# Expert weights in 16 KB runs: gate and up as whole matrices, with the contraction permuted to match

## The reference

```python
lg = jnp.einsum('nd,dg->ng', xn, rg_w) + rg_b          # group of 4, top 1
le = (jnp.einsum('nd,de->ne', xn, re_w) + re_b).reshape(-1, N_GROUPS, EXPERTS_PER_GROUP)
...                                                     # top 2 of the 8 experts in it
for e in range(N_EXPERTS):
    hdn = jax.nn.silu(xn @ w_gate[e]) * (xn @ w_up[e])  # 1024 x 512 each
    out = out + combine[:, e:e + 1] * (hdn @ w_down[e]) # 512 x 1024
return x + out
```

## Time and profile before

| | us |
|---|---|
| median of 3 runs | 843.48 |
| the profiled execution | 843.39 |
| its span | 841.6 |
| TensorE matmuls busy | 775.0 (92%) |
| VectorE busy | 427.2 (51%) |
| ScalarE busy | 324.3 (39%) |
| TensorE waiting for `exp_w_up` transfers | 26.3 |
| SP weight transfers, issue to landing, median | 25.9 to 26.9 |

### The profile page before, as it was taken

How to read it: one execution, slowest core, us unless ns; L and a number is a source line. 1 busy time by engine, 2 the same in 40 slices (tenths; PEclk the granted TensorE clock), 3 DMA queues, 4 the chain that set the end, 5 groups by cost and what they waited for, 6 DMA issues and landing times.

```text
span 841.6 us, 21589 instructions
## 1 busy us (share of the span) xinstructions
PE 775.0 (92%) x8655; PEld 591.7 (70%) x8656; DVE 427.2 (51%) x1142; ACT 324.3 (39%) x562; POOL 259.1 (31%) x132
## 2 busy tenths in 40 slices
PE   4999999999999999999999979999898889989964
PEld 4999999999999999865555545555555545545532
DVE  3156977999994244153444333445343334434424
ACT  4432767564345833253323322323322223222224
POOL 3846699978577778200000000000000000000000
PEclk9999999999999999989999999999999999999997
DMA  7734343435454746963899999999999999999992
GB/s 254 229 106 145 101 151 100 151 100 160 129 180 158 280 150 241 339 278 151 340 422 423 421 422 422 422 421 422 422 422 421 422 422 422 421 422 423 421 421 119
DMA packets 53173, 249.99 MB, mean 297 GB/s; under 512 B 6600, under 2 KB 6600, under 8 KB 28562
## 3 DMA queue, kind: packets, MB, share of 16 engines
q1 hardware_dynamic: 49760, 246.95, 74.1%
q10 hardware_dynamic: 3377, 2.57, 1.2%
HBM read 246.76 MB, written 2.75 MB: 296 GB/s over the span
## 4 chain that ended last, share of the span: by engine, by line
PE 62%; DMA 18%; DVE 11%; SPq 4%; ACT 2%; issue 2%; ACTq 1%; DVEq 0%
PE bank L1450 24%; DMA piece<-in_exp_w_up 17%; PE bank L1621 12%; DVE bank L1065 7%; PE bank L1650 7%; PE bank L1572 5%; PE bank L1609 4%; PE bank L1448 4%; SPq L549 4%; PE bank L1637 1%; DVE sq L1127 1%; PE bank L1579 1%; PE bank L1519 1%; DMA stage<-in_norm_g 1%; PE bank L1513 1%
## 5 line engine op out<-in xcount | busy, mean ns | idle before, releaser
L603 POOL TENSOR_TENSOR w_lo<-raw,w_hi 128x2048 fp32r<-128x2048 f32 x39 | 180.5, 4631 | 62.6 <-ACT w_hi L728 62.5
L1621 PE MATMUL bank<-piece,xe 128*32 128x256 f32 x2816 | 169.5, 392 | 32.1 <-DMA piece<-in_exp_w_up 26.3
L1621 PEld LDWEIGHTS bank<-piece,xe 128*32 128x32 f32 x2816 | 97.7, 113 | 98.0 <-issue 47.5
L1450 PE MATMUL bank<-x_hi,w_hi 128*128 128x384 f32 x432 | 145.4, 337 | 0.3 <-DVE ua L1084 0.2
L1450 PE MATMUL bank<-x_hi,w_lo 128*128 128x384 f32 x432 | 144.4, 334 | 0.0
L1450 PE MATMUL bank<-x_lo,w_hi 128*128 128x384 f32 x432 | 144.4, 334 | 0.0
L1065 DVE SCALAR_TENSOR_TENSOR bank<-ub,vec,bank 128x256 f32<-128x256 f32 (+1 forms) x416 | 137.2, 419 | 0.0
L1296 DVE SCALAR_TENSOR_TENSOR silu_and_hid<-bank,few,silu_and_hid 64x256 f32<-64x256 f32 x44 | 21.5, 490 | 170.4 <-ACT silu_and_hid L914 170.4
L728 ACT ACTIVATE w_hi<-raw 128x2048 fp32r<-128x2048 f32 x39 | 74.8, 1919 | 74.8 <-PE bank L1450 71.2
L1650 PE MATMUL bank<-piece,hidT 128*32 128x256 f32 x1408 | 94.2, 384 | 5.5
L1450 PEld LDWEIGHTS bank<-x_hi,w_hi 128*128 128x128 f32 x432 | 81.1, 188 | 1.4 <-DVE ua L1084 0.5
(11 more groups left out here) (239 smaller groups left out, 1009.9 us busy)
## 6 DMA issues: line engine op xcount, KB each, us to landing
piece<-in_exp_w_down SPq DMA_DIRECT2D x64, 1024.0 KB, 26.6
piece<-in_exp_w_gate SPq DMA_DIRECT2D x64, 1024.0 KB, 25.9
piece<-in_exp_w_up SPq DMA_DIRECT2D x64, 1024.0 KB, 26.9
raw<-in_w_in SPq DMA_DIRECT2D x28, 1024.0 KB, 5.2
raw<-in_w_out_a SPq DMA_DIRECT2D x4, 1024.0 KB, 5.0
raw<-in_w_out_b SPq DMA_DIRECT2D x4, 1024.0 KB, 5.3
raw<-in_w_o SPq DMA_DIRECT2D x4, 1024.0 KB, 5.0
out<-n_out SPq DMA_DIRECT2D x3, 512.0 KB, 3.3
```

What stands on the lines that cost most here:

```text
L603: pool.tensor_tensor(w_lo[u % NW][:, :, :], raw[u % NW][:, :, :], w_hi[u % NW][:, :, :].bitcast(F32), ALU.subtract).then_inc(lo_ready, 1)
L1450: ins = pe.matmul(b, wp[:, k % UK, cols], xp[:, k, :], start=start, stop=stop)
L1621: last = pe.matmul(GU[q * T:(q + 1) * T, :], xe[:, k, :], wide(pairs[q // 2], k)[:, q % 2 * QE:(q % 2 + 1) * QE], start=(k == 0), stop=(k ...
```

## The change

Gate and up of a side get one buffer of 16 KB per partition each, `matrix{n}`, which covers two adjacent pieces; down keeps its two pieces. The numbers in `SETS` change so that the two pieces of gate, and of up, are adjacent. In memory a matrix is now read as one contiguous block of 2 MiB in which partition `p` holds rows `8p` to `8p+7`, one run of 16 KB. Block `k` of the contraction is made of the rows `8 p + k`, and `by_row` and the load of `norm2_g` follow. For the first four experts each matrix is still loaded as two transfers of 8 KB per partition, now with a distance of 16 KB between the runs in memory. From the fifth expert on gate and up are one transfer each. `gate_up_half` is gone: both are issued on `gate_up_done`, and TensorE waits for both whole matrices in front of the first of its 64 matmuls.

```diff
-    SETS = (((15, 16), (17, 18), (20, 9)), ((10, 11), (12, 1), (2, 0)),
-            ((4, 7), (5, 8), (3, 6)), ((13, 14), (19, 21), (22, 23)))
+    SETS = (((16, 17), (10, 11), (15, 18)), ((0, 1), (4, 5), (9, 12)),
+            ((2, 3), (6, 7), (8, 13)), ((20, 21), (22, 23), (14, 19)))
...
+        matrix = {s[c][0]: at(f"matrix{s[c][0]}", [P, 4096], F32, halves_at + UNIT * s[c][0]) for s in SETS for c in range(2)}
...
-        w_gu = {0: w_gate.rearrange("l e (h p j) c -> (l e) h p (j c)", h=2, p=P),
-                1: w_up.rearrange("l e (h p j) c -> (l e) h p (j c)", h=2, p=P)}
+        w_gu = {0: w_gate.rearrange("l e (p j) c -> (l e) p (j c)", p=P), 1: w_up.rearrange("l e (p j) c -> (l e) p (j c)", p=P)}
...
-            return t.rearrange("p (h q j) -> p h j q", h=2, q=P)
+            return t.rearrange("p (q j) -> p j q", q=P)
...
-            return piece[pair[k // RJ]][:, :].rearrange("p (j c) -> p j c", j=RJ)[:, k % RJ, :]
+            return matrix[pair[0]][:, :].rearrange("p (k c) -> p k c", k=KB)[:, k, :]
...
-                for c, h in ((0, 0), (1, 0), (0, 1), (1, 1), (2, 0), (2, 1)):
-                    n = SETS[side][c][h]
-
-                    used = (down_half, down_done) if c == 2 else (gate_up_half, gate_up_done)
-                    sp.wait_ge(used[h], last_item)
-                    src = w_dn if c == 2 else w_gu[c]
-                    sp.dma_start(piece[n][:, :], src[bass.ds(e, 1), h, :, :].rearrange("e p x -> p (e x)"))\
+                sp.wait_ge(gate_up_done, last_item)
+                for c in range(2):
+                    n = SETS[side][c][0]
+                    sp.dma_start(matrix[n][:, :], w_gu[c][bass.ds(e, 1), :, :].rearrange("e p x -> p (e x)"))\
+                      .then_inc(weights_in[n], 16)
+                for h, done in enumerate((down_half, down_done)):
+                    n = SETS[side][2][h]
+                    sp.wait_ge(done, last_item)
+                    sp.dma_start(piece[n][:, :], w_dn[bass.ds(e, 1), h, :, :].rearrange("e p x -> p (e x)"))\
                       .then_inc(weights_in[n], 16)
...
-                for part, done in enumerate((gate_up_half, gate_up_done)):
-                    pe.wait_ge(weights_in[pairs[0][part]], filled)
-                    pe.wait_ge(weights_in[pairs[1][part]], filled)
-                    for k in range(part * KB // 2, (part + 1) * KB // 2):
+                pe.wait_ge(weights_in[pairs[0][0]], filled + 16)
+                pe.wait_ge(weights_in[pairs[1][0]], filled + 16)
+                for k in range(KB):
...
-                    last.then_inc(done, 1)
+                last.then_inc(gate_up_done, 1)
```

More of the change, by code:

```diff
@@ L56, in trunk_program @@
     HALF = 512
-    SETS = (((15, 16), (17, 18), (20, 9)), ((10, 11), (12, 1), (2, 0)),
-            ((4, 7), (5, 8), (3, 6)), ((13, 14), (19, 21), (22, 23)))
+    SETS = (((16, 17), (10, 11), (15, 18)), ((0, 1), (4, 5), (9, 12)),
+            ((2, 3), (6, 7), (8, 13)), ((20, 21), (22, 23), (14, 19)))
+    assert all(a % 2 == 0 and b == a + 1 for s in SETS for a, b in s[0:2])
     NSETS = len(SETS)
@@ L357, in trunk_program @@
         xe_ready = sem("xe_ready")
-        gate_up_half = sem("gate_up_half")
         gate_up_done = sem("gate_up_done")
@@ L481, in _, with first_weights @@
             sp.dma_start(x_tok[:, NP // P, :], x_sample.rearrange("s t d -> (s t) d")).then_inc(x_sample_in, 16)
[L483 to L488, removed]
+            FIRST = {SETS[e][c][h]: (e, c, h) for e in range(NSETS) for c in range(3) for h in range(2)}
+            def first_weights(*pieces):
+                for n in pieces:
+                    e, c, h = FIRST[n]
+                    if c == 2:
+                        sp.dma_start(piece[n][:, :], w_dn[e, h]).then_inc(weights_in[n], 16)
+                    else:
+                        m = SETS[e][c][0]
+                        sp.dma_start(matrix[m][:, h * 2048:(h + 1) * 2048], w_gu[c][e][:, h * 2048:(h + 1) * 2048])\
+                          .then_inc(weights_in[m], 16)
+            TAPS_USED = {32: 15, 33: 16, 34: 17, 35: 18}
             X_LO_USED = CHUNKS.index(("gB", 1))
@@ L491, in _ @@
                 if u == 30:
-                    first_weights(0, 2, 0)
+                    first_weights(20)
                 if u == 1:
@@ L503, in _ @@
                     sp.wait_ge(tails_ready, 2 + 4 * KB)
-                    first_weights(0, *TAPS_USED[u])
+                    first_weights(TAPS_USED[u])
             sp.wait_ge(grp_done, CHUNK_END[X_LO_USED])
-            first_weights(0, 2, 1)
+            first_weights(9)
             sp.wait_ge(grp_done, CHUNK_END[NCH - 3])
-            first_weights(1, 0, 0)
-            first_weights(1, 0, 1)
-            first_weights(1, 1, 0)
+            first_weights(10, 11, 12)
             sp.wait_ge(lo_ready, UNITS - 2)
-            first_weights(1, 1, 1)
+            first_weights(1)
             sp.wait_ge(lo_ready, UNITS - 1)
-            first_weights(1, 2, 0)
+            first_weights(2)
             sp.wait_ge(lo_ready, UNITS)
-            first_weights(1, 2, 1)
+            first_weights(0)
             sp.wait_ge(grp_done, CHUNK_END[NCH - 2])
-            first_weights(2, 0, 0)
-            first_weights(2, 0, 1)
+            first_weights(4, 7)
             sp.wait_ge(half_done, NCH)
-            first_weights(2, 1, 0)
-            first_weights(2, 1, 1)
+            first_weights(5, 8)
             sp.wait_ge(grp_done, len(GROUPS))
[L525 to L528, removed]
+            first_weights(3, 6, 13, 14)
             sp.wait_ge(aux_done, aux("logit", NT - 1) + 1)
-            first_weights(3, 1, 0)
+            first_weights(19)
             sp.wait_ge(stage_out[0], 80)
@@ L864, in _ @@
             act.dma_start(rw[:, :, NG:R], expert_w.rearrange("l (k p) g -> p (l k) g", p=P)).then_inc(rw_in, 16)
-            act.dma_start(norm2_by_row[:, :].rearrange("p (h j) -> p h j", h=2),
-                          norm2_g.rearrange("l (h p j) -> p (l h) j", h=2, p=P)).then_inc(rw_in, 16)
+            act.dma_start(norm2_by_row, norm2_g.rearrange("l (p j) -> p (l j)", p=P)).then_inc(rw_in, 16)
             act.dma_start(rbias[:, 0:NG], group_b.to_broadcast([P, NG])).then_inc(rw_in, 16)
@@ L878, in rows_in_blocks @@
             def rows_in_blocks(i):
-                act.activation(x_rows[:, i, :].rearrange("p (h j q) -> p h j q", h=2, j=RJ), by_row(x_tok[:, i, :]),
+                act.activation(x_rows[:, i, :].rearrange("p (j q) -> p j q", j=KB), by_row(x_tok[:, i, :]),
                                ACT.Copy).then_inc(x_rows_ready, 1)
@@ L1615, in item @@
                 pe.wait_ge(xe_ready, i + 1)
-                for part, done in enumerate((gate_up_half, gate_up_done)):
-                    pe.wait_ge(weights_in[pairs[0][part]], filled)
-                    pe.wait_ge(weights_in[pairs[1][part]], filled)
-                    for k in range(part * KB // 2, (part + 1) * KB // 2):
[L1620 to L1623, removed]
-                    last.then_inc(done, 1)
+                pe.wait_ge(weights_in[pairs[0][0]], filled + 16)
+                pe.wait_ge(weights_in[pairs[1][0]], filled + 16)
+                for k in range(KB):
+                    for q in range(TILES):
+                        last = pe.matmul(GU[q * T:(q + 1) * T, :], xe[:, k, :],
+                                         wide(pairs[q // 2], k)[:, q % 2 * QE:(q % 2 + 1) * QE],
+                                         start=(k == 0), stop=(k == KB - 1))
+                last.then_inc(gate_up_done, 1)
                 pe.wait_ge(picked, i + 2)
```

6 lines of the change are left out of this document (1 added, 5 removed).

## The result

The changed kernel takes 845.37 us in the median of 14 runs (841.98 to 846.39), the kernel before 843.61 in 14 runs beside them (843.2 to 844.99). The ratio is 1.0016, with a 95% interval of 1.0008 to 1.0023: slower by 0.16%, some 1.4 us. The forecast was 842.5, a gain of 0.9. The profiled execution took 844.6 us with a span of 842.8 (before: 843.39 and 841.6).

The account below looks back on a forecast made before the run. The prediction took the expert stage's weight stream as the bound, with TensorE's work behind its last gate/up bytes. From 843.39 it added 1.72 (start), -4.4 (rate), 1.73 (tail) and 0.1 (small edits): 842.5 us, range 839.8 to 846.9.

Parts of the forecast that it names:

- What bounds the kernel: Expert stage: the weight stream's start, its bytes at its rate, and TensorE's work after the last gate/up bytes set the end.
- Start of the stream, +1.72: SP's refill of expert side 1 at 417.21 goes out 1.72 us later, since it waits for `gate_up_done`.
- Rate of the stream, -4.4: Over 27 experts, 18 packets' fixed cost of 9 ns is saved per expert and engine: 4.4 us gained.
- After the last gate/up bytes, +1.73: Last item: 32 more of the 64 matmuls move behind the last landing, 1.71 to 1.73 us.
- I take the same loss of 1.8 us, so no term: Last item: TensorE's low clock after the wait costs 1.8 us as before, so nothing is added.
- Rival (a): TensorE's clock holds in the tail, 1.8 us less: 840.7; chance 0.14.
- about 1.8 more: Last item, far end of the clock's effect: low clock through all 64 matmuls, about 1.8 us more.
- Small edits, +0.1: TensorE's register instruction ahead of the down matmuls costs 0.02 us in each of five items; other edits hidden or unchanged.
- (d): Rival: the strided `x_rows` copy ahead of the logits doubles in time: 845.6; chance 0.04.
- (c): Rival: a 16 KB run moves at the rate of two 8 KB runs, no stream gain: 846.9; chance 0.14.
- (b): Rival: a packet's fixed part is larger, 11 to 15 ns; 840.6 at 13, 831.8 at 31; chance 0.20.
- Sum: Whole kernel: 843.39 + 1.72 - 4.4 + 1.73 + 0.1 = 842.5 us.

Follow-up runs that it names:

- run 3: The base with each later gate or up matrix loaded by two transfers of 8 KB runs instead of one of 16 KB; 848.18 us, ratio 1.0054 to the kernel before.
- run 5: Changed kernel with weight counts in registers, and the 32nd expert's gate and up in halves; 841.07 us, ratio 0.9964 to the kernel before.
- run 6: Changed kernel with weight counts in registers, and experts 5 and 6 refilled in early halves; 842.24 us, ratio 0.9981 to the kernel before.
- run 9: Changed kernel with weight counts in registers, and 24 extra matmuls in the wait ahead of the last item; 842.48 us, ratio 0.9977 to the kernel before.
- run 8: Changed kernel with weight counts in registers, early half refills of experts 5 and 6, last expert in halves; 840.86 us, ratio 0.9965 to the kernel before.
- run 12: The kernel of run 5 measured again; 841.75 us, ratio 0.9969 to the kernel before.
- run 11: The kernel of run 8 measured again; 840.41 us, ratio 0.9957 to the kernel before.
- the base: Changed kernel with TensorE's loop bounds taken through a maximum with zero; 844.5 us, ratio 1.001 to the kernel before.
- run 10: The kernel of run 8 with 16 extra matmuls between the two halves of the last item; 840.4 us.

## Why the prediction was wrong

- **What bounds the kernel**: right. The end follows the start of the stream, its rate and the tail; runs 3, 5, 6 and 9 each moved one of these and the total with it.
- **Start of the stream, +1.72**: right. Run 6 takes it away and gains 1.8 in the ratios, 1.35 at the last landing of its trace. The trace of the changed kernel shows +2.25: 0.4 more belong to the register instruction in three items, and 0.1 to the first item.
- **Rate of the stream, -4.4**: the first step that failed, as a size. The mechanism is right (run 3), but a packet spared is worth 0.14 us / 18 = 7.8 ns, not 9, and the gain is 3.8. I took the middle between 4 and 13 ns, from landings of lone transfers. (The records of single packets say 12 ns, but the overlap between packets takes a part of it back.) The rule on the page of the Trainium skill (DMA: Bandwidth & Descriptors, Why small descriptors are slow), by which the estimate was 3.5 ns, does not agree with the runs: it would have made 1.7 us. The two sources stood on either side of the value. I also wrote that packets fall by a third. In 500 to 600 they fall from 5796 to 3939, a third indeed, over the whole program by 15%.
- **After the last gate/up bytes, +1.73**: the second step that failed, and the larger. The 1.7 us of matmuls are right (21.4 against 23.1 at full clock). "I take the same loss of 1.8 us, so no term" was the error. The measured losses are 2.8, 1.6, 2.8, 1.7, 1.7 and 1.9 us (the tail, less 23.1) in the six traces that await whole matrices with no extra work in the wait, 2.1 in the mean, never zero. With halves (less 21.4) they are 1.6, 0, 0 and 1.7 in the traces of runs 5, 8, 12 and 11, and 1.7 in that of the kernel before, 1.0 in the mean. So some traces of both kinds have the same loss; but halves escaped it in two traces of five, and whole matrices in none of six. Why is in part my reading: with twice as many matmuls behind the wait, more of them can be caught at the low clock, and the wait in front is no longer broken by 32 matmuls (0.87 granted in it, before it was 1.00). The length of the wait does not order the losses: 5.55 us idle and 1.9 lost in run 6, 3.90 idle and 2.8 lost in the changed kernel. Nor was the wait one of about 5.5 us: the 64 matmuls of item 43 lost some of the clock too (5.20 us at 802.26 instead of 3.64), which leaves 3.90. Rival (a), that the clock holds, pointed the other way, and was wrong. I had named the loss of "about 1.8 more" as an end of the range and not as a case with a chance of its own.
- **Small edits, +0.1**: the third step that failed, as a size, since I put the register instruction low without a row for it. It costs 0.13 to 0.14 us in each item, not 0.02. Of the 44 items only the three ahead of item 4, which releases side 1, and the last one can pass that on to the end: 0.5. `x_rows` stayed at 2.04 to 2.17 us per copy, so (d) is out. (c) is out by run 3. (b) is out by the 7.8 ns.
- **Sum.** Put right, the terms are 1.7 for the start, -3.8 for the rate, 1.7 for the matmuls of the tail, 0 to 1.1 in a trace for the clock beyond the loss of before, and 0.5 for the register instructions: +0.1 to +1.2. Measured were +1.4 (interval 0.7 to 1.9) and +0.8 in the base (0.1 to 1.6). The forecast was made of two losses of 1.7 and a gain of 4.4 that nearly cancel, so that errors of 0.6, 0.4 and 1 us, all to one side, were enough to turn the sign. The time was within the range, which for a sum that says faster where it was slower is luck.

## What to carry to other kernels

Where a stream of transfers sets the end, coarser transfers gain at each one, by the fixed cost of the packets saved, and lose at the two ends: the first can't start before its whole buffer is free, and the last must land whole before any work on it starts. Make the middle coarse and the two ends fine. And count the engine's clock with the work that stands behind the last landing: work behind a wait may run at half speed, so moving it there can cost more than its duration (here 4.5 instead of 1.7 us, in the worst traces).

## What the runs showed of the hardware

- A run of 16 KB per partition is moved as one packet, which takes 614.8 ns in the mean, where one of 8 KB takes 313.5. In the pace of the stream a packet spared is worth 7.8 ns: 14.77 against 14.91 us per expert of 6 MiB.
- TensorE came out of a wait at 1.2 or at 2.4 GHz in two executions of one kernel, after 2.29 and 2.27 us of idle time (runs 5 and 12). The first item of the expert stage does the same at the other end. Each is worth 1.1 to 1.7 us of 844.
- A sum ahead of a wait on TensorE took 0.13 us of its queue in each item, and the profile puts it down to the engine that the next wait names.
- Four instruction packets of 16 KB among the weight transfers in the 35 us ahead of the last landing went with a landing 1.5 us later; five in an earlier stretch went with 0.15 us. Whether they are the cause is open.
- float32 matmuls on two, three or four different column tiles took the same 0.43 us (runs 10, 9 and the real 64).
